# Expert weights in an encoder layer: second matrix of each expert loaded from ScalarE's queue, first one as its slots come free, and the last second-matrix product moved to other banks

## The reference

```
h2      = rmsnorm(x2) * norm_ffn
top_v, top_i = top_k(h2 @ w_router + b_router, 4);  gate = softmax(top_v)
for each block of rows that go to one expert e:
    gu  = xb @ w_gate_up[e] + b_gate_up[e]         # 1024 x 2048, 8 MiB
    g   = min(gu[:, :1024], 7);  lin = clip(gu[:, 1024:], -7, 7)
    act = g * sigmoid(1.702 * g) * (lin + 1)
    y   = act @ w_down[e] + b_down[e]              # 1024 x 1024, 4 MiB
x2[token] += gate * y          # summed over a token's four experts
out = rmsnorm(x2) * norm_final
```

## Time and profile before

| | us |
|---|---|
| median of three runs | 1465.5 |
| lowest, highest | 1463.52, 1466.69 |
| profiled execution | 1465.08 |
| its span | 1463.2 |
| TensorE busy | 1431.0 (98% of the span) |
| weight loads of TensorE | 752.4 |
| VectorE busy | 499.0 |
| ScalarE busy | 323.9 |
| GpSimd busy | 276.9 |
| bytes moved by DMA | 466.72 MB, 319 GB/s over the span |

### The profile page before, as it was taken

One profiled execution on the slowest core, in us unless ns is written; L12 is line 12 of the kernel. 1 busy time (PEld: TensorE's weight loads), 2 busy tenths in 40 slices (PEclk: granted clock), 3 DMA queues, 4 the chain that ended last, 5 costly groups with the idle time before them and its releaser, 6 DMA issues.

```text
span 1463.2 us, 34048 instructions
## 1 busy us (share of the span) xinstructions
PE 1431.0 (98%) x14854; PEld 752.4 (51%) x14854; DVE 499.0 (34%) x715; ACT 323.9 (22%) x556; POOL 276.9 (19%) x360
## 2 busy tenths in 40 slices
PE   8999999999989999999999999999999999999997
PEld 7876588888863444444444444444444443333334
DVE  4848833324572223222222222232222222222233
ACT  6458842223121111111111111111111111111111
POOL 0000000000012222233222233222332222332211
PEclk9999999999999999999999999999999999999999
DMA  7330003323969599999999999999999999999987
GB/s 260 146 94 1 23 12 123 96 73 134 362 237 418 215 415 418 414 417 412 413 420 414 416 416 411 417 414 418 418 412 414 417 418 418 418 414 413 416 338 254
DMA packets 77595, 466.72 MB, mean 319 GB/s; under 512 B 23160, under 2 KB 31764, under 8 KB 52944
## 3 DMA queue, kind: packets, MB, share of 16 engines
q1 hardware_dynamic: 50528, 448.83, 74.4%
q0 software_dynamic: 18464, 16.94, 5.3%
q10 hardware_dynamic: 8560, 0.34, 0.3%
HBM read 456.69 MB, written 19.27 MB: 325 GB/s over the span
## 4 chain that ended last, share of the span: by engine, by line
PE 81%; DMA 14%; DVE 3%; issue 1%; ACT 1%; SPq 0%; POOL 0%; ACTq 0%; DVEq 0%; POOLq 0%
PE ps L1783 35%; PE ps L1799 19%; DMA dn_pair<-in_w_down 11%; PE ps L1433 7%; PE ps L1435 7%; PE ps L1434 7%; PE ps L1460 2%; DMA gu_pair<-in_w_gate_up 2%; PE ps L1586 1%; DVE head_max L1092 1%; PE ps L1542 1%; DVE probs L1110 1%; DMA xf<-x_rows 1%; DMA x_rows<-y_sb,sum_row 0%; PE ps L1689 0%
## 5 line engine op out<-in xcount | busy, mean ns | idle before, releaser
L1783 PE MATMUL ps<-gu_pair,xt 128*32 128x512 f32 x6144 | 668.4, 594 | 4.1 <-ACT ps L861 3.0
L1783 PEld LDWEIGHTS ps<-gu_pair,xt 128*32 128x32 f32 x6144 | 204.2, 110 | 448.0 <-issue 427.6
L1799 PE MATMUL ps<-dn_pair,act_t 128*32 128x256 f32 x6144 | 339.2, 379 | 2.5 <-DMA dn_pair<-in_w_down 2.0
L1799 PEld LDWEIGHTS ps<-dn_pair,act_t 128*32 128x32 f32 x6144 | 203.3, 110 | 146.6 <-issue 13.5
L1332 DVE TENSOR_SCALAR lin_sb<-ps 128x768 f32<-128x768 f32 x32 | 30.6, 958 | 584.7 <-ACT sg_sb L852 584.7
L852 ACT ACTIVATE sg_sb<-ps,limits 128x768 f32<-128x768 f32 x32 | 28.8, 901 | 593.5 <-PE ps L1783 593.5
L954 POOL DMA_INDIRECT x_rows<-y_sb,sum_row x93 | 147.0, 1581 | 37.7 <-issue 37.7
L931 POOL TENSOR_TENSOR mark_sb<-ones 1x1 f32<-1x1 f32 x93 | 30.0, 323 | 613.8 <-DVE y_sb L1348 608.7
L1433 PE MATMUL ps<-w_high,h_hi 128*128 128x512 f32 x352 | 138.2, 392 | 0.6 <-DVE mem_lo L1038 0.5
L1435 PE MATMUL ps<-w_high,h_lo 128*128 128x512 f32 x352 | 137.2, 390 | 0.0
L1434 PE MATMUL ps<-w_low,h_hi 128*128 128x512 f32 x352 | 137.0, 389 | 0.0
(11 more groups left out here) (249 smaller groups left out, 1002.6 us busy)
## 6 DMA issues: line engine op xcount, KB each, us to landing
gu_pair<-in_w_gate_up SPq DMA_DIRECT2D x128, 2048.0 KB, 29.0
dn_pair<-in_w_down SPq DMA_DIRECT2D x64, 2048.0 KB, 19.9
w_raw<-in_w_in SPq DMA_DIRECT2D x8, 2048.0 KB, 7.9
w_raw<-in_w_out SPq DMA_DIRECT2D x2, 2048.0 KB, 8.0
w_raw<-in_w_in SPq DMA_DIRECT2D x2, 1024.0 KB, 8.1
x_sb<-in_x SPq DMA_DIRECT2D x8, 256.0 KB, 7.8
w_raw<-in_w_mem_kv SPq DMA_DIRECT2D x1, 2048.0 KB, 12.6
x<-in_x SPq DMA_DIRECT2D x4, 512.0 KB, 5.3
```

The source lines that it names most:

```text
L1783: last = nc.tensor.matmul(ps[quarter(q), g, :], xt[:, g, k, :], w.rearrange("p (h n) -> p h n", h=2)[:, :, q * QCOLS:(q + 1) * QCOLS], sta ...
L1799: last = nc.tensor.matmul(ps[quarter(q), bank + g, 0:QCOLS], act_part(2 * c + h, g), dn_w[c][:, h * D + q * QCOLS:h * D + (q + 1) * QCOLS] ...
```

## The change

SyncE's loop now issues first matrices alone, each load at the part that frees its slot; the first two matrices after the start are written out ahead of the loop. The second matrices are issued from ScalarE's queue, after the seed of the following job, with the same waits as before. The last activation is turned into a buffer of its own, `last_act_t`, directly after it is made. The last `down` writes banks 0 to 2 instead of 4 to 6 and waits only for the `take_y` two jobs before it (argument `free`); the down biases of the first token block go to banks 4 to 7 inside it, after its third part. The token blocks use the other four banks each (`4 - 4 * (t % 2)`), and TensorE waits for all of `y_lo_last` before it overwrites banks 0 to 3.

```diff
--- before.py
+++ after.py
@@ -271,6 +271,7 @@
         xg = [sb(f"xg{i}", [P, D], F32, (166 + 4 * i) * KIB) for i in range(2)]
         xq = [sb(f"xq{i}", [P, TRIOS, QCOLS], F32, (166 + 4 * i) * KIB) for i in range(2)]
         act_t = sb("act_t", [P, KD * SLOTS], F32, 174 * KIB)
+        last_act_t = sb("last_act_t", [P, KD * SLOTS], F32, 170 * KIB)
         lin_sb = sb("lin_sb", [P, TRIOS, QCOLS], F32, 177 * KIB)
         sg_sb = sb("sg_sb", [P, TRIOS, QCOLS], F32, 180 * KIB)
         act_sb = sb("act_sb", [P, KD * SLOTS], F32, 184 * KIB)
@@ -628,23 +629,25 @@
             sp.wait_ge(gate_t_ps, 1)
             load_gu(e_one, 1, GU_PAIRS - 1)
             pairs_but_one = sp.value_load(job_table[0:1, 1, 1:2], min_val=MIN_PAIRS - 1, max_val=NJ // 2 - 1)
-            with sp.Fori(0, pairs_but_one) as i:
+
+            def next_gu(i, b, e_gu):
+                for m in range(GU_PAIRS):
+                    wait_part(sp, i, b * PARTS - DN_PARTS + 2 * m + 1)
+                    load_gu(e_gu, b, m)
+
+            e_two = sp.value_load(job_table[0:1, 0, 2:3], min_val=0, max_val=N_EXP - 1)
+            for m in range(GU_PAIRS):
+                wait_part(sp, 0, 2 * m + 1)
+                load_gu(e_two, 0, m)
+            e_three = sp.value_load(job_table[0:1, 0, 3:4], min_val=0, max_val=N_EXP - 1)
+            next_gu(0, 1, e_three)
+            with sp.Fori(1, pairs_but_one) as i:
                 for b in range(2):
                     e_gu = sp.value_load(job_table[0:1, 0, bass.ds(i * 2 + b + 2, 1)], min_val=0, max_val=N_EXP - 1)
-                    e_dn = sp.value_load(job_table[0:1, 0, bass.ds(i * 2 + b + 1, 1)], min_val=0, max_val=N_EXP - 1)
-                    for m in range(GU_PAIRS):
-                        wait_part(sp, i, b * PARTS + 2 * m + 1)
-                        load_gu(e_gu, b, m)
-                    for m in range(DN_PAIRS):
-                        wait_part(sp, i, stream(b, KD + 2 * m + 1))
-                        load_dn(e_dn, m)
-            e_last = sp.value_load(job_table[0:1, 0, bass.ds(pairs_but_one * 2 + 1, 1)], min_val=0, max_val=N_EXP - 1)
+                    next_gu(i, b, e_gu)
             wait_part(sp, pairs_but_one, stream(0, KD - 1))
             for t in range(TB):
                 sp.dma_start(down_bias[N_EXP * t:N_EXP * (t + 1), :], b_down[0]).then_inc(down_bias_in, 16)
-            for m in range(DN_PAIRS):
-                wait_part(sp, pairs_but_one, stream(0, KD + 2 * m + 1))
-                load_dn(e_last, m)
             sp.wait_ge(act_ready, pairs_but_one * 2 + 2)
             sp.dma_start(final_gain[:], norm_final.rearrange("(a n) -> a n", a=1).to_broadcast([P, D])).then_inc(fgain_in, 16)
             sp.wait_ge(added, pairs_but_one * (32 * TRIOS) + (16 + 16 * TRIOS))
@@ -860,6 +863,9 @@
                     act.wait_ge(gs_ready, j)
                 nc.scalar.activation(ps[:, 0:TRIOS, :], bias_sb[:].rearrange("p (a h) n -> p a (h n)", a=1).to_broadcast([P, TRIOS, COLS]),
                                      ACT.Copy).then_inc(seeded, 1)
+
+            def next_dn(e, m):
+                act.dma_start(dn_pair[m][:], wdn[e, m, :, :]).then_inc(dn_in[m], 16)
 
             def keep_gate(j, b):
                 nc.scalar.activation(y_gate[:, b:b + 1, :], slot_gates[:, bass.ds(j, 1), :], ACT.Copy).then_inc(gate_kept, 1)
@@ -892,10 +898,18 @@
                     wait_part(act, i, stream(b, KD - 1))
                     sigmoid(j + 1)
                     seed(j + 2)
+                    e_dn = act.value_load(job_table[0:1, 0, bass.ds(j + 1, 1)], min_val=0, max_val=N_EXP - 1)
+                    for m in range(DN_PAIRS):
+                        wait_part(act, i, stream(b, KD + 2 * m + 1))
+                        next_dn(e_dn, m)
             keep_gate(pairs_but_one * 2, 0)
             act.wait_ge(act_ready, pairs_but_one * 2 + 1)
             wait_part(act, pairs_but_one, stream(0, KD - 1))
             sigmoid(pairs_but_one * 2 + 1)
+            e_last = act.value_load(job_table[0:1, 0, bass.ds(pairs_but_one * 2 + 1, 1)], min_val=0, max_val=N_EXP - 1)
+            for m in range(DN_PAIRS):
+                wait_part(act, pairs_but_one, stream(0, KD + 2 * m + 1))
+                next_dn(e_last, m)
             act.wait_ge(y_ready, pairs_but_one * 2 + 1)
             keep_gate(pairs_but_one * 2 + 1, 1)
             nc.scalar.activation(mark_act[:], ones[0:1, 0:1], ACT.Sqrt).then_inc(last_gate_kept, 1)
@@ -903,7 +917,7 @@
             act.wait_ge(gate_kept, pairs_but_one * 2 + 2)
             wait_part(act, pairs_but_one, stream(0, PARTS + DN_PARTS - 1))
             for g in range(TRIOS):
-                nc.scalar.activation(y_hi_last[:, g, :], ps[:, 4 + g, 0:QCOLS], ACT.Copy,
+                nc.scalar.activation(y_hi_last[:, g, :], ps[:, g, 0:QCOLS], ACT.Copy,
                                      scale=y_gate[:, 1, g:g + 1]).then_inc(y_hi_ready, 1)
             for t in range(TB):
                 if t < TB - 1:
@@ -911,7 +925,7 @@
                     rows = xf[:, t, :].rearrange("p (h n) -> p h n", h=4)
                 else:
                     act.wait_ge(last_ps, TB)
-                    rows = ps[:, 4:8, 0:QCOLS]
+                    rows = ps[:, 0:4, 0:QCOLS]
                 nc.scalar.activation(xf_squares[:].rearrange("p (h n) -> p h n", h=4), rows, ACT.Square,
                                      accum_out=f_ss[:, t:t + 1]).then_inc(fsq_done, 1)
                 act.wait_ge(fsq_done, t + 1)
@@ -1380,6 +1394,7 @@
             clamp(pairs_but_one * 2 + 1)
             activate(pairs_but_one * 2 + 1)
             dve.wait_ge(act_ready, pairs_but_one * 2 + 2)
+            nc.vector.transpose(last_act_t[:], act_sb[:]).then_inc(act_t_done, 1)
             dve.wait_ge(rows_kept, pairs_but_one * 4 + 3)
             for t in range(TB):
                 nc.vector.tensor_scalar(last_row[:, t, :], sum_row[:, 1, :], cols[:, 5:6], -4.0 * P * t, ALU.subtract, ALU.add).then_inc(last_row_ready, 1)
@@ -1389,14 +1404,13 @@
                     nc.vector.tensor_scalar(token_hot[:, g, t, :], counter[:], 4.0, last_row[:, t, g:g + 1], ALU.mult,
                                             ALU.is_equal).then_inc(token_hot_ready, 1)
             wait_part(dve, pairs_but_one, stream(0, PARTS - 1))
-            turn_act(pairs_but_one * 2 + 1)
             take_y(pairs_but_one * 2, 0)
 
             dve.wait_ge(act_t_done, pairs_but_one * 2 + 2)
             dve.wait_ge(gate_kept, pairs_but_one * 2 + 2)
             for g in range(TRIOS):
                 dve.wait_ge(y_hi_ready, g + 1)
-                nc.vector.scalar_tensor_tensor(out=y_lo_last[:, g, :], in0=ps[:, 4 + g, 0:QCOLS], scalar=y_gate[:, 1, g:g + 1],
+                nc.vector.scalar_tensor_tensor(out=y_lo_last[:, g, :], in0=ps[:, g, 0:QCOLS], scalar=y_gate[:, 1, g:g + 1],
                                                in1=y_hi_last[:, g, :].bitcast(F32), op0=ALU.mult, op1=ALU.subtract).then_inc(y_lo_ready, 1)
             dve.wait_ge(fgain_in, 16)
 
@@ -1404,7 +1418,7 @@
                 dve.wait_ge(xf_in[t], 16)
                 dve.wait_ge(last_ps, t + 1)
                 v = xf[:, t, :].rearrange("p (h n) -> p h n", h=4)
-                nc.vector.tensor_tensor(v, v, ps[:, 4 * (t % 2):4 * (t % 2) + 4, 0:QCOLS], ALU.add).then_inc(xf_ready, 1)
+                nc.vector.tensor_tensor(v, v, ps[:, 4 - 4 * (t % 2):8 - 4 * (t % 2), 0:QCOLS], ALU.add).then_inc(xf_ready, 1)
 
             def inverse(t):
                 dve.wait_ge(frt_ready, t + 1)
@@ -1422,7 +1436,7 @@
             inverse(TB - 1)
             for n in range(2):
                 cols_n = slice(n * COLS, (n + 1) * COLS)
-                nc.vector.scalar_tensor_tensor(out=xf[:, TB - 1, cols_n].rearrange("p (h n) -> p h n", h=2), in0=ps[:, 4 + 2 * n:6 + 2 * n, 0:QCOLS],
+                nc.vector.scalar_tensor_tensor(out=xf[:, TB - 1, cols_n].rearrange("p (h n) -> p h n", h=2), in0=ps[:, 2 * n:2 * n + 2, 0:QCOLS],
                                                scalar=f_rstd[:, TB - 1:TB], in1=final_gain[:, cols_n].rearrange("p (h n) -> p h n", h=2),
                                                op0=ALU.mult, op1=ALU.mult).then_inc(out_ready, 1)
 
@@ -1766,9 +1780,9 @@
 
                 return slice(QUARTER * q, QUARTER * (q + 1))
 
-            def act_part(k, g):
-
-                return act_t[:, k * SLOTS + QUARTER * g:k * SLOTS + QUARTER * (g + 1)]
+            def act_part(a, k, g):
+
+                return a[:, k * SLOTS + QUARTER * g:k * SLOTS + QUARTER * (g + 1)]
 
             def gate_up(j, s, loads, between):
 
@@ -1786,9 +1800,9 @@
                     last.then_inc(gemm_ps, 1)
                     between(k)
 
-            def down(j, bank, between):
-
-                pe.wait_ge(y_ready, j + 1)
+            def down(j, bank, a, free, between):
+
+                pe.wait_ge(y_ready, free)
                 pe.wait_ge(act_t_done, j + 1)
                 for c in range(DN_PARTS):
                     if c % 2 == 0:
@@ -1796,7 +1810,7 @@
```

(21 more changed lines are left out.)

## The result

The changed kernel took 1471.3 us (median of 6 runs, 1469.9 to 1471.7) beside 1465.1 us for the kernel before (6 runs). The ratio of the two is 1.0037, with a 95% interval of 1.0026 to 1.0047: a small slowdown, but clear of the noise. I had predicted 1457.6.

The account below looks back on a forecast made before the run. TensorE was taken to bound the earlier jobs, transfers the last ones. From 1465.08 us, 6.95 for the loop and 0.9 for the end came off, giving 1457.2; with 0.4 for the median, 1457.6 us, range 1455.5 to 1474.

Parts of the forecast that it names:

- The gap and the first matrices: DMA idle from 476.5 to 491.7 us: first-matrix loads issued up to 10.4 us earlier would fill it.
- the whole 6.95 us of the loop: Time lost to transfers in the last eight or nine jobs, all claimed to come back.
- The second matrices: Loads from ScalarE's own queue: two take 21 us at most, inside the limit of about 25.9 us.
- an equal share is enough: Second-matrix queue: with every second turn, a load of 5.28 us takes 10.6 us, within the limit.
- GpSimd's transfers: Scatters and gathers sharing with two large queues: delayed 0 to 10.6 us per job, taken as 4.5, which just fits.
- the occupancy of 26.5 us: GpSimd's transfers, first scatter to last gather: 26.5 us of a 30.96 us job, leaving 4.4 us free.
- the ring: Found afterwards, in the loop: `take_y`, third scatter's issue 5.75 us later, its landing, next `take_y`; 33.0 us when slow.
- Rival 3: Scatters and gathers become the loop's bound past 4.4 us added delay per job: 1473 us, chance 0.25.
- the 19 us: In the loop, `take_y` may be late by about 19 us before TensorE feels it.
- The end: After job 30's down product: the 0.98 us turn moves ahead; gain taken as 0.9 us, from 0 to 1.0.
- Rival 1: Transfers served in order of arrival, so ScalarE's loads stand behind SyncE's: 1463.5 us, chance 0.10.
- rival 2: Transfer rate falls by 2.2% with two large streams, some 5.5 us return as waits: 1463 us, chance 0.10.

Follow-up runs that it names:

- e9: Kernel before with all loads in SyncE's queue, four first-matrix loads ahead of the second matrix in early jobs, two later; old end: 1461.1 us, ratio 0.9969.
- e15: Changed kernel with only the second-matrix loads written as two halves of 1 MiB each: 1481.3 us, ratio 1.0107 to the kernel before.
- e1: Kernel before with only the loop's part of the change, its end as it was: 1475.4 us, ratio 1.0066.
- e6: Kernel before with only the second matrices moved to ScalarE's queue, first matrices still late, old end: 1478.6 us, ratio 1.0097.
- e11: Changed kernel with the last second matrix loaded into first-matrix slots free since job 30's: 1464.3 us, ratio 0.9988 to the kernel before.
- e3: Kernel before with first matrices loaded as their slots come free, all loads kept in SyncE's queue, old end: 1467.9 us, ratio 1.0019.
- e12: Changed kernel with each 2 MiB load written as two of 1 MiB: 1472.1 us, ratio 1.0045 to the kernel before.

## Why the prediction was wrong

**The gap and the first matrices: right.** The share is 1.01, the loads were done early, and the profile of e9 shows that the whole 6.95 us of the loop are there to be had, with jobs of 30.96 us to the end. One reading was too simple: not every late job of the kernel before had a second-matrix load in its chain. At 1338.26 us it is a first-matrix load, of 29.64 us.

**The second matrices: right in the changed kernel.** They never stand in the chain before the last one. The guess that an equal share is enough held only while both queues have equal rows (e15).

**GpSimd's transfers: the step that failed.** "I take 4.5 us, which just fits." By its own sum it did not even fit: 4.4 us were free. The bounds were right, 0 to 10.6 us; the value was not. The third scatter came 8.5 us later in the changed kernel (26.3 against 17.8) and 9.5 in e1. I had let half of the second-matrix loads pass ahead of the scatters. But by the prediction's own sum the two last 21 us when they take turns, from 5.2 us before the end of down on, and the scatters start 2 us after it: two thirds lie beside them, 7 us. The limit was also another one than the occupancy of 26.5 us with the gathers in it: the ring leaves 30.96 - 5.75 - 17.8 = 7.4 us. So even the right limit, wider than my 4.4, was passed. Rival 3 had the place and the sign. That its 1473 us lies near the measured 1471.3 is partly luck: it had the drift use up all of the 19 us, which happened in e1 and e6, not in the changed kernel.

**The 19 us that `take_y` may be late: wrong for the changed kernel.** There TensorE feels it at 10 us, by the stalls inside the down product. They make up the 0.6 us per job from 963.64 us on, with the ring and TensorE at nearly one period. e1, whose loop has the same instructions, had no stall and went past this: `take_y` came 20 us late before TensorE felt it, close to my 19, and then the ring took 16.6 us. Why one stays and the other goes on I cannot say.

**The end: wrong in sign.** I had moved the turn (0.98 us) and called the last down product "held by its weights", yet left its price as it was. In the profile before, its first load was issued 6.75 us before the end of down of job 30 (1425.68 against 1432.43), because a transfer wait stretched that product. At TensorE's own pace it is 5.2 us, a load takes 9.2 to 9.5, and the wait grows from 2.5 to 4.5 us and takes the clock with it. So the end came out 2.7 us longer instead of 0.9 shorter. e11 removes the wait, and the end is 7.2 us shorter.

**Rival 1 and rival 2** did not show in the changed kernel: no second-matrix load is in its chain before the last one, and its rate from 600 to 1000 us is that of the kernel before, 415 GB/s. Waiting in order of arrival showed in e3, with one queue, and a lower rate in e12, where the rows are halved.

## What to carry over

A small indirect transfer pays in turns: count its rows per DMA engine, multiply by the time of one row of each large queue that is active beside it, and compare the ring it belongs to with the period of the loop. Before a queue is added to keep one kind of load from waiting, try another order in the queue that is there: here four loads ahead of the second matrix while the backlog is small and two once it has grown took every load out of the chain (0.9969, and 0.9927 with the new end and the last weights loaded early). When a stall is removed, recompute every later wait at the new pace, since a wait's start may have been set by the stall.
